# PEER queries of a hybrid decoder layer: w_q streamed 512 columns wide by tokens, and turned afterwards

## The reference

```python
def peer_ffn(h, w_q, keys1, keys2, u_tab, v_tab):          # h = RMSNorm(x), 512 x 1024
    q = (hf @ w_q).reshape(tokens, PEER_HEADS, 2, PEER_HALF)  # 8 heads x 2 x 128
    s1 = einsum('thd,hnd->thn', q[:, :, 0], keys1)            # 128 scores each
    s2 = einsum('thd,hnd->thn', q[:, :, 1], keys2)
    v1, i1 = top_k(s1, 16); v2, i2 = top_k(s2, 16)
    ...                                                       # best 16 of 16 x 16 pairs, softmax gate
    # per token 8 x 16 = 128 experts: act = gelu(u_row . h), y += gate * act * v_row
```

## Time and profile before

| | |
|---|---|
| median of 3 executions | 1775.87 us |
| the profiled execution: own time / span | 1784.04 / 1782.3 us |
| TensorE matmul / weight load busy | 78% / 46% |
| VectorE, ScalarE, GpSimd busy | 59%, 19%, 44% |
| moved by the gathers | 536.92 MB of 599.48 MB |
| mean granted TensorE clock | 0.871 |

### The profile page before, as it was taken

One profiled execution on the slowest core, in us unless ns is written; L12 is line 12 of the kernel. 1 busy time (PEld: TensorE's weight loads), 2 busy tenths in 40 slices (PEclk: granted clock), 3 DMA queues, 4 the chain that ended last, 5 costly groups with the idle time before them and its releaser, 6 DMA issues.

```text
span 1782.3 us, 17771 instructions
## 1 busy us (share of the span) xinstructions
PE 1392.8 (78%) x5982; PEld 818.0 (46%) x5982; DVE 1046.3 (59%) x2839; ACT 344.2 (19%) x778; POOL 778.4 (44%) x848
## 2 busy tenths in 40 slices
PE   8999987678677978696765768667787887877777
PEld 7898657555344656474322546112233333333333
DVE  5633379256654588777655536454465666666653
ACT  3222321112223231101100001010122212222121
POOL 3000026256555556666656365655444343333331
PEclk9999989789787889777879789769989998899889
DMA  4224548579987999999999798999999999999995
GB/s 167 72 95 159 208 142 294 213 293 412 378 321 287 338 403 389 347 337 385 412 403 410 274 351 308 369 413 417 417 422 421 422 421 422 420 423 421 421 422 224
DMA packets 130315, 599.48 MB, mean 336 GB/s; under 512 B 15920, under 2 KB 15920, under 8 KB 97456
## 3 DMA queue, kind: packets, MB, share of 16 engines
q0 software_dynamic: 115776, 536.92, 76.5%
q1 hardware_dynamic: 14256, 61.15, 8.9%
q10 hardware_dynamic: 192, 0.26, 0.0%
HBM read 596.18 MB, written 2.10 MB: 336 GB/s over the span
## 4 chain that ended last, share of the span: by engine, by line
PE 41%; DMA 27%; issue 9%; DVE 8%; another core or an unknown queue 7%; ACT 3%; POOL 3%; DVEq 1%; ACTq 0%; SPq 0%; POOLq 0%
DMA arena<-in_peer_uv,arena 19%; PE psum L1093 8%; PE psum L1037 7%; DMA arena<-in_peer_v,arena 6%; PE psum L1074 5%; PE psum L784 5%; PE psum L782 3%; DVE arena L1815 3%; POOL arena L718 2%; PE psum L1018 1%; PE psum L902 1%; PE psum L895 1%; POOL arena L706 1%; PE psum L824 1%
## 5 line engine op out<-in xcount | busy, mean ns | idle before, releaser
L1815 DVE CUSTOM_DVE_ANT_0 arena<-arena,psum 128x1024 f32<-128x1024 f32 x512 | 622.0, 1217 | 377.1 <-DMA arena<-in_peer_uv,arena 228.1
L1093 PE MATMUL psum<-arena 128*128 128x512 f32 x896 | 438.2, 647 | 94.2 <-ACT arena L1363 94.2
L706 POOL DMA_INDIRECT arena<-in_peer_u,arena x288 | 273.6, 950 | 384.5 <-PE psum L847 221.4
L718 POOL DMA_INDIRECT arena<-in_peer_v,arena x288 | 273.4, 949 | 247.7 <-PE psum L1074 119.0
L738 POOL DMA_INDIRECT arena<-in_peer_uv,arena x220 | 206.9, 940 | 323.8 <-PE psum L1093 289.3
L1093 PEld LDWEIGHTS psum<-arena 128*128 128x128 f32 x896 | 180.7, 207 | 356.1 <-issue 225.4
L1074 PE MATMUL psum<-arena 128*32 128x512 f32 x1152 | 244.6, 740 | 87.6 <-DMA arena<-in_peer_v,arena 59.0
L1037 PE MATMUL psum<-arena 128*128 128x128 f32 x1024 | 133.2, 288 | 51.5 <-issue 50.5
L1037 PEld LDWEIGHTS psum<-arena 128*128 128x128 f32 x1024 | 126.9, 202 | 61.7 <-issue 61.5
L1074 PEld LDWEIGHTS psum<-arena 128*32 128x32 f32 x1152 | 43.5, 123 | 237.3 <-issue 126.3
L1363 ACT ACTIVATE arena<-arena 128x128 f32<-128x128 f32 x224 | 71.5, 390 | 309.8 <-DVE arena L1801 273.1
(11 more groups left out here) (256 smaller groups left out, 1411.9 us busy)
## 6 DMA issues: line engine op xcount, KB each, us to landing
arena<-in_w_in SPq DMA_DIRECT2D x28, 1024.0 KB, 4.9
arena<-in_w_out SPq DMA_DIRECT2D x16, 512.0 KB
arena<-in_peer_w_q SPq DMA_DIRECT2D x16, 512.0 KB
arena<-in_peer_w_q SPq DMA_DIRECT2D x8, 1024.0 KB
arena<-in_peer_u,arena POOLq DMA_INDIRECT x292, 5.8
arena<-in_peer_v,arena POOLq DMA_INDIRECT x292, 21.5
arena<-in_peer_uv,arena POOLq DMA_INDIRECT x220, 27.4
arena<-in_x SPq DMA_DIRECT2D x4, 512.0 KB, 5.1
```

Source lines behind the costliest of these rows:

```text
L706: pool.indirect_dma_start(row, None, u_d, bass.IndirectOffsetOnAxis(ap=eid[i % 2][:, c:c + 1], axis=0)).then_inc(landed, 16)
L718: pool.indirect_dma_start(row, None, v_d, bass.IndirectOffsetOnAxis(ap=eidT[k % (2 * PH // UH)][:, at_:at_ + 1], axis=0)).then_inc(landed, 16)
L1093: mm = pe.matmul(bank[y_bank[i][half]], diag_w[q % 2][:, j], row[:, D + half * 512:D + (half + 1) * 512], start=False, stop=c == SEL - 1, ...
L1815: dve.tensor_tensor_reduce(row, row, h2p[i], 1.0, 0.0, ALU.mult, ALU.add, dots[:, c:c + 1]).then_inc(s["u_free"], 1)
```

## The change

Fourteen of the sixteen `q` steps (all but tile 0's first two) swap the operands: the 8 blocks of turned tokens are the weights, and 512 columns of `w_q` stream past each, 8 matmuls of 512 columns. The result has tokens on the partitions, so ACT copies it to `qs`, a new step `qt` turns the four 128 x 128 pieces with four TensorE transposes, and ACT copies them back over `qs`. `s` now waits for `qt`'s copy. The steps are put in another order so that something else stands between a `q` and its `qt`, and a `qt` and its `s`, where the list allows.

```diff
 def route(t):
-    return [("h2T", t, 0), ("h2T", t, 1), ("q", t, 0), ("q", t, 1), ("s", t, 0), ("q", t, 2), ("s", t, 1),
-            ("q", t, 3), ("s", t, 2), ("s", t, 3)]
+    return [[("h2T", t, 0)], [("h2T", t, 1)], [("q", t, 0)], [("qt", t, 0), ("q", t, 1)], [("s", t, 0), ("qt", t, 1), ("q", t, 2)],
+            [("s", t, 1), ("qt", t, 2), ("q", t, 3)], [("s", t, 2), ("qt", t, 3)], [("s", t, 3)]]
+def by_tokens(t, i):
+    return t > 0 or i > 1
...
-LAST_QUERIES = {26: ("q", 0, 3), 27: ("s", 0, 3), 28: ("q", 1, 2), 29: ("s", 1, 2), 30: ("q", 1, 3), 31: ("s", 1, 3)}
+LAST_QUERIES = {26: [("q", 0, 3)], 27: [("qt", 0, 3)], 28: [("s", 0, 3), ("q", 1, 2)], 29: [("qt", 1, 2)],
+                30: [("s", 1, 2), ("q", 1, 3)], 31: [("qt", 1, 3)], 32: [("s", 1, 3)]}
...
-    for j, step in enumerate(route(2)):
-        at.setdefault(END + 9 + 3 * j, []).append(step)
+    for j, some in enumerate(route(2)):
+        at.setdefault(END + 9 + 3 * j, []).extend(some)
...
-        at.setdefault(END + 38 + 2 * j, []).append(step)
+    for j, some in enumerate(route(3)):
+        at.setdefault(END + 37 + 3 * j, []).extend(some)
...
-                    for j in range(4 * i, 4 * i + 4):
+                    if by_tokens(t, i):
                         for c in range(DC):
                             w = w_q_s[c] if t >= GT else w_q_h[i // 2][c]
-                            at_ = j if t >= GT else j % (NS // 2)
+                            at_ = 4 * i if t >= GT else 4 * (i % 2)
+                            mm = pe.matmul(ps, h2T[t][:, c], w[:, at_ * HALF:(at_ + 4) * HALF], start=c == 0, stop=c == DC - 1)
...
+                elif kind == "qt":
+                    ps = claim("qt", t, i)
+                    pe.wait_ge(*read("q", t, i))
+                    for j in range(4):
+                        mm = pe.transpose(ps[:, j * P:(j + 1) * P], qs[t % 2][:, 4 * i + j], ident[:])
+                    mm.then_inc(filled("qt", t, i)[0], 1)
...
-                    pe.wait_ge(*read("q", t, i))
+                    pe.wait_ge(*read("qt" if by_tokens(t, i) else "q", t, i))
...
+                elif kind == "qt":
+                    act.wait_ge(*filled("qt", t, i))
+                    act.copy(qs[t % 2][:, 4 * i:4 * i + 4], heads(bank_for("qt", t, i))).then_inc(read("qt", t, i)[0], 1)
```

More of the change, by code:

```diff
@@ L220, in first_group @@
     out += [("q", 0, 1), ("s", 0, 1), ("mix", 1, 0), ("mix", 1, 1), ("wo", 1, 0), ("wo", 1, 1), ("add", 1, 0), ("add", 1, 1),
-            ("n2", 1, 0), ("xsq", 1, 0), ("q", 0, 2), ("s", 0, 2)]
-    return out + [("h2T", 1, 0), ("h2T", 1, 1), ("q", 1, 0), ("s", 1, 0), ("q", 1, 1), ("s", 1, 1)]
+            ("n2", 1, 0), ("xsq", 1, 0), ("q", 0, 2)]
+    return out + [("h2T", 1, 0), ("h2T", 1, 1), ("qt", 0, 2), ("q", 1, 0), ("s", 0, 2), ("qt", 1, 0), ("q", 1, 1),
+                  ("s", 1, 0), ("qt", 1, 1), ("s", 1, 1)]
 HELD = {("st", 1, 0): 1, ("add", 1, 0): 8, ("add", 1, 1): 8, ("n2", 1, 0): 8}
-LAST_QUERIES = {26: ("q", 0, 3), 27: ("s", 0, 3), 28: ("q", 1, 2), 29: ("s", 1, 2), 30: ("q", 1, 3), 31: ("s", 1, 3)}
+LAST_QUERIES = {26: [("q", 0, 3)], 27: [("qt", 0, 3)], 28: [("s", 0, 3), ("q", 1, 2)], 29: [("qt", 1, 2)],
+                30: [("s", 1, 2), ("q", 1, 3)], 31: [("qt", 1, 3)], 32: [("s", 1, 3)]}
 def second_group():
@@ L283, in places @@
     steps = second_group()
-    for n, step in LAST_QUERIES.items():
-        at.setdefault(n, []).append(step)
+    for n, some in LAST_QUERIES.items():
+        at.setdefault(n, []).extend(some)
     at.setdefault(SCALE_AT, []).append(("xsc", 1, 0))
@@ L293, in places @@
     at.setdefault(END + 1, []).append(("n2", 2, 0))
-    for j, step in enumerate(route(2)):
-        at.setdefault(END + 9 + 3 * j, []).append(step)
+    for j, some in enumerate(route(2)):
+        at.setdefault(END + 9 + 3 * j, []).extend(some)
     at.setdefault(END + 26, []).append(("n2", 3, 0))
-    for j, step in enumerate(route(3)):
-        at.setdefault(END + 38 + 2 * j, []).append(step)
+    for j, some in enumerate(route(3)):
+        at.setdefault(END + 37 + 3 * j, []).extend(some)
     return at
@@ L320, in banks_of @@
         return [(a, b)[i if kind == "h2T" else "qs".index(kind)]]
-    if kind in ("h2T", "q", "s"):
+    if kind in ("h2T", "q", "qt", "s"):
         return [turn % 4]
@@ L1032, in step_ @@
                         pe.wait_ge(s["wq_in"], 16 * DC * (3 if t >= GT else 1 + i // 2))
-                    for j in range(4 * i, 4 * i + 4):
+                    if by_tokens(t, i):
                         for c in range(DC):
                             w = w_q_s[c] if t >= GT else w_q_h[i // 2][c]
-                            at_ = j if t >= GT else j % (NS // 2)
+                            at_ = 4 * i if t >= GT else 4 * (i % 2)
+                            mm = pe.matmul(ps, h2T[t][:, c], w[:, at_ * HALF:(at_ + 4) * HALF], start=c == 0, stop=c == DC - 1)
+                    for j in range(4 * i, 4 * i + 4) if not by_tokens(t, i) else []:
+                        for c in range(DC):
+                            w, at_ = w_q_h[0][c], j
                             mm = pe.matmul(ps[:, j % 4 * P:(j % 4 + 1) * P], w[:, at_ * HALF:(at_ + 1) * HALF], h2T[t][:, c],
```

## The result

| | before | changed |
|---|---|---|
| median of 15 executions, same chip | 1781.78 us | 1764.47 us |
| their spread | 1764.41 to 1805.27 | 1750.86 to 1779.42 |
| profiled execution: own time / span | 1784.04 / 1782.3 | 1751.1 / 1749.4 |

The ratio is 0.9913 with a 95% interval of 0.9886 to 0.9941: 15.5 us, where 36 were forecast. The time lies in the predicted range, and inside the 1% that I had called no change. The two profiled executions differ by 33 us, near the 37 of the prediction's sum, but that is chance: the changed kernel's was the second fastest of its 15. The changed kernel is faster, clear of noise, but by less than half of what was forecast.

The account below looks back on a forecast made before the run. TensorE's query matmuls stutter under full DMA load and ACT's order holds up DVE, stopping gathers in two troughs; 1784.0 - 20 - 13 - 7 + 3 = 1747 us profiled, 1740 timed; range 1724 to 1779 us.

Parts of the forecast that it names:

- Number of records: Wide queries need 40 instead of 128 TensorE records per step, ending the stutter of "issue" waits; 20 and 13 us.
- second trough: Slices 22 to 25 (980 to 1158 us): 13 us gained from the stutter, 7 from order, 3 lost.
- Added work: Fourteen `qt` steps and hand-overs on TensorE and ACT: 3 us lost in the second trough, between 0 and 6.
- rival 2: Half the gain: first trough closes, second does not, or the stutter returns in other steps; 1759 us, chance 0.10.
- First trough: Slice 7 (312 to 356 us): stutter ends, first gelu near 330, DVE's 20.6 us wait goes; 20 us, 0 to 20.6.
- The order's 7: Second trough: ACT does `load_h2(2)` before tile 3's first query, cutting DVE's 16.4 us wait to about 4; 7 us gained.
- Earlier `w_in`: First trough: SP's `w_in` loads for the next stage, which follow the last query, start 21 us sooner; no separate size.
- Rival 1: Stutter not caused by the number of records, or absent in timed runs, so only order counts; 1773 us, chance 0.25.
- Rival 3: Wide queries run at the low granted clock because of idle hand-overs and transposes around them; 1804 us, chance 0.10.

Follow-up runs that it names:

- quarter_again: Changed kernel with each wide matmul cut into four of 128 columns, so 64 + 64 records per query; ratio to before 1.0117.
- no_turn: Changed kernel with the `qt` steps left out, so scores come from unturned queries and other experts are chosen; ratio to before 0.9783.
- after_again: Changed kernel once more without any edit, for a second trace; ratio to before 0.9934.
- first_only: Changed kernel with tiles 2 and 3 kept in the narrow form and old order; ratio to before 0.9986.
- gelu_first_wide: Changed kernel with the first gelu put ahead of the turning and scores of tile 1's last two queries; ratio to before 0.9844.
- order_only: Kernel before with tile 3's first query one place later, so `load_h2(2)` goes ahead of it; ratio to before 1.0045.
- queries_first_wide: Changed kernel with the first gelu ahead of the last turnings and the last three queries run one behind the other; ratio to before 0.9870.

## Why the prediction was right in its mechanism and wrong in size

1. **Number of records: right in the sum.** 36 us (`quarter_again` against the changed kernel), 38.6 with the order but no turning (`no_turn`). The prediction had 20 + 13 for this. That the sum fits so well is in part luck, for its parts do not: between the traces of `quarter_again` and the two of the changed kernel 10 to 15 us arise by row 34 (20 forecast), 8 to 12 between the troughs (none forecast) and 14 to 32 in the second trough (13 forecast). What the engine lacks in the stutter stays open: an "issue" wait names nothing. The Trainium skill (Runtime: NRT & Kernel Launch, Instruction fetch mechanics) calls instruction fetch mostly hidden; by that rule these gains would be zero, and only on the one chip without a stutter were they. The page fits there, and elsewhere the measurement decides against zero, though it doesn't prove that fetch is the cause; no instruction packet runs during the stutter.

2. **Added work: the step that failed.** The sum had 3 us for turning in the second trough and a hand-over at 0.72 us in the first. The runs show 21 to 27 us. The 15.5 us can be split in two ways. `quarter_again` has the turning, the new order and the old number of records, and lies 21 us above before (12 to 30 by its interval), which leaves 36 for the records. `no_turn` has the records and the order and lies 38.6 below (29 to 48), which leaves 23 for the turning, or 27 against `after_again`. One prices the turning, with the order, among narrow records, the other among wide ones, on different chips, and they agree. I counted each hand-over at what it takes with ACT at once at work (the 0.72 us of the earlier trace rows), though the earlier trace rows showed a copy 9.54 us late for no named reason, which I used only for rival 2. Under full DMA engines ACT's copies after a query were up to 14 us late, and turning adds one such dependence per query right in TensorE's path. That these waits are the price fits the eight traces in the table above; why the copies are late stays open.

3. **First trough, 20: measured about 9.** DVE's wait fell from 20.6 to 11.4 us; the leads at row 34 are 8.6, 13.6 and 12.8, less 0 to 4 by which before itself scatters, and the timed runs of `first_only` show only 2.5 (-4 to 9). Without turning it is 9 to 13. The forecast let the gelu follow the last `qt` at 330; the late copy moved it to 342.32. Putting the gelu ahead of that copy brings what was missing (19.1 at row 34 in `gelu_first_wide`).

4. **Second trough, 13 + 7 - 3: measured between -0.4 and +17.9** in the two traces of the changed kernel, +24.9 without turning. The order's 7 is 0 by itself or less (`order_only`, 8 us slower).

5. **Earlier `w_in`: nothing seen**, by `queries_first_wide`, where it came 11.7 us sooner. I had named it as a second thing that hangs on the last query; it carried no number.

6. **Rivals.** Rival 1 (not the number of records) fell on the chips of 1780 us and holds on the other. Rival 2, a second trough held back by ACT's delays and the new hand-overs, is what happened, with a first trough only half closed besides; its 1759 is nearest to 1764. Rival 3, the clock, is not seen: wide queries took 7.03 us, or 8.84 behind a wait of 11 us, 7.3 on the mean of all fourteen, and the mean clock rose from 0.871 to 0.879. In the 11 us wait itself the clock fell to 0.5, so what little the clock cost came from the wait. Its sum was off besides: 1776 + 28 leaves out rival 1's gain; with it, it is 1801.

7. **One argument was void.** Against rival 1 I held that an artefact of the profiler would set the profiled execution apart from the timed ones. Every timed execution here was recorded in the same way, so the comparison could not tell. Whether an unrecorded execution stutters is not shown; that a recorded one need not is (the chip of 1663 us). The same holds for ACT's late copies.

## What to carry to other kernels

Where gathers filled the DMA engines, a long dense run of small matmuls made TensorE stutter on all chips but one; the same columns in a quarter of the instructions ran clean. But each new hand-over between engines in such a stretch needs a bound from the longest wait of its kind in the trace, not from the usual one alone. Then ask which single wait holds the gathers' rings, and see whether moving that one instruction does it more cheaply: here the gelu's place gave 7 us to the kernel before and about 12 to the changed one, with no new work.

## What the runs showed of the hardware that I had not expected

- The same kernel takes 1663 us on one chip and 1777 to 1782 on the four others, with 410 GB/s against 310 to 405 in the stage that mixes gathers with matrix work; in the stage of gathers alone both move 421.
- On the slower chips executions of the kernel before scatter over 36 us (1761.42 to 1797.2 in 35), on the fast one over 7 (in 23).
- An ACT copy came 6 to nearly 14 us after TensorE had written its bank while the DMA engines were full (308.3 to 314.38 in the changed kernel, 311.9 to 325.60 in `no_turn`); on the fast chip the query of 303.52 ended at 310.55 and was copied at 310.59.
- Four float32 transposes and two idle hand-overs around every wide query did not lower the granted clock: it is 1.00 from 298 to 315.2 us in the changed kernel, with 16 records in 7.03 us at 308.18, right behind them.
- With wide matmuls TensorE ran three queries, 48 records, without a pause inside a query while 395 GB/s were moved (`queries_first_wide`, 302.4 to 323.5 us), in the stretch where narrow ones stutter.
